# Forgetting attention on one core: the transposes of the inverse sums and the product that spreads them get fixed places behind a tile's scores

## The chip, the core and the metric

The kernel runs as one program on 1 core of one Trainium2 chip. The number that counts is the device time of the whole kernel in microseconds (us). It was run three times before the change, and once more under the profiler.

## What is computed

Two transformer blocks run one behind the other over 1024 tokens of width 1024, in fp32. The second block's mixer holds the part that the change touches, a causal attention with 8 heads of 64 and a forgetting bias, beside a pooling branch:

```python
def forgetting_attention(q, k, v, f_logit):
    ...
    log_f = jax.nn.log_sigmoid(f_logit.astype(jnp.float32)).transpose(0, 2, 1)
    cf = jnp.cumsum(log_f, axis=-1)
    ...
        s = jnp.einsum('bhqd,bhkd->bhqk', qb, k, preferred_element_type=jnp.float32) * scale
        s = s + cq[..., :, None] - cf[..., None, :]
        s = jnp.where(kpos[None, :] <= qpos[:, None], s, NEG_INF)
        p = jax.nn.softmax(s, axis=-1)
        return jnp.einsum('bhqk,bhkd->bhqd', p.astype(v.dtype), v)
```

The rest (retention, window attention, the two MLPs, norms, projections) is long rows of matrix products that the change leaves alone.

## The kernel before

Each engine has its own program, written out by hand, and the programs meet only at semaphores. Products are kept exact to fp32 by splitting operands into a high and a low part.

**Units and items.** The attention is cut into 16 units `u`. Unit `u` belongs to item `idx = u // 2`; items 0 to 7 are (pair of heads `t`, query half `Q`) = (0,0), (0,1), (1,0), and so on, and `j = u % 2` is the head of the pair. So even items have 4 blocks of keys per unit and odd items 8. All engines walk the same list, `attention_order`: 17 steps `s`, each of 4 slots `ii`. In a slot come, in this order, the scores of the tile (128 queries) that follows, the weights of tile (`s`, `ii`), and then, for unit `s - 1`, one turn (even item) or two turns (odd item).

- scores: TensorE (PE) writes them to PSUM (L1049 to L1051), VectorE (DVE) takes their minimum (L2397).
- weights: ScalarE (ACT) takes the exponential into `Pu` (L1667) and adds up the rows into `st`; this frees the scores' bank.
- turn `n`: PE transposes up to 4 blocks of `Pu` into a PSUM bank (L1062), ACT copies that bank to `PAh` (L1675), DVE subtracts to get `PAl` (L2402) and frees the bank. Two turns later PE multiplies `PAh` and `PAl` with the values (L1078, L1079).

**The ring of two banks.** Turns use PSUM banks 4 and 5 in rotation. So a turn's transposes wait for the `PAl` of the turn before the last one, unless something else takes a place in the rotation between them.

**The tail.** When a unit's last values are issued, a generator `tail(u)` starts, and each later turn on each engine takes it one step further. It normalizes the item:

- the first unit of an item, first step on DVE: `inverse`, four small operations (L2415, L2418, L2422, L2423), turns the 8 sums into inverses and packs them into `n4`.
- second step: ACT copies half of the product to `ot` (L1687), DVE adds it to the other half (L2435).
- third step, first unit: PE takes the next bank of the rotation ("nT") and transposes `n4` into it (L1095, 4 transposes, called **the transposes** below); ACT copies the bank to `rw` (L1693) and frees it.
- third step, second unit: PE takes the next bank ("rl") and spreads `rw` over 128 rows with one product (L1103, **the product** below); DVE multiplies the item's output with it (L2440, **the multiplication**) and frees the bank. GpSimd (POOL) then splits the output into `chi` and `clo` (L2659, L2661), in a queue with the operand splits for later pairs of heads (`stack`, L2618 to L2630).

Of the kernel before, what the change touches and what calls it, by code (L numbers as in the profile page):

```python
# [9 lines left out]
ACT = mybir.ActivationFunctionType  # L10
ALU = mybir.AluOpType
# [54 lines left out]
class Tally:  # L66
# [24 lines left out]
    def ok(self, *name):  # L91
        if not self.building:
            return None, 1
        topic, count = self.value[name]
        return self.sem(topic), count
# [110 lines left out]
def idle(n):  # L206

    for _ in range(n):
        yield


def run(gen):
    for _ in gen:
        pass
# [145 lines left out]
ITEMS = [(t, Q) for t in range(4) for Q in range(2)]  # L360
# [9 lines left out]
    return max(0, k - 4 * ITEMS[u // 2][1])  # L370


def attention_order(scores, weights, stack, turned, values, tail, pooled):

    restack, tails = iter(()), []
    scores(0, 0)
    n = 0
    for s in range(17):
        if s % 4 == 1 and s < 12:
            restack = stack(s // 4 + 1)  # L380
        for ii in range(4):
            if 4 * s + ii + 1 < 64:
                scores(*divmod(4 * s + ii + 1, 4))
            if s < 16:
                weights(s, ii)
            next(restack, None)
            if s == 0:
                pooled(ii)
            for _ in range(1 + ITEMS[(s - 1) // 2][1] if s else 0):
                turned(n, *TURNS[n])  # L390
                if n >= LAG:
                    values(n - LAG, *TURNS[n - LAG])
                    if TURNS[n - LAG][0] < TURNS[n - LAG + 1][0]:
                        tails.append(tail(TURNS[n - LAG][0]))
                for g in tails:
                    next(g, None)
                n += 1
    for m in range(n - LAG, n):
        values(m, *TURNS[m])
    tails.append(tail(15))  # L400
    for g in tails:
        run(g)
def build(nc, I, out, sg, cd, yd, xd, ud):
    with ExitStack() as ctx:
        return programs(nc, ctx, I, out, sg, cd, yd, xd, ud)


def programs(nc, ctx, I, out, sg, cd, yd, xd, ud):
    wp, x_in, rows, sinks, bf, ps = (I[n] for n in ("wp_d", "x_d", "rows_d", "sinks_d", "bf_d", "ps_d"))
    cst, swab, poolw, wf = (I[n] for n in ("cst_d", "swab_d", "pw_d", "wf_d"))  # L410
    tally = Tally(nc, ctx)
    up, ok = tally.up, tally.ok
# [5 lines left out]
    def bank_of(*group):  # L418
        return bank[tally.banks[group]]

    def free(*group):

        return tally.sem(f"free{tally.banks[group]}"), 1
# [11 lines left out]
    ident = at("ident", CO, [128, 128])  # L435
# [153 lines left out]
    ov = [at(f"ov{i}", WO + 28 + 2 * i, [128, 512]) for i in range(2)]  # L589
    ot = at("ot", XO + 28, [128, 512])  # L590
    rw = at("rw", XO + 30, [34, 512], F32R)
    sel = at("sel", FO + 72.625, [34, 128], F32R)
    chi4 = at("chi4b", FO, [128, T], F32R)
    nh = at("nh", FO + 72, [128, 8], F32R)
    n4 = at("n4", FO + 72.0625, [128, 136])
# [10 lines left out]
    def unit_of(u):  # L606

        idx, j = divmod(u, 2)
        return (idx, j) + ITEMS[idx]
# [20 lines left out]
    def tensor_program(e):  # L630
        ring = Ring(tally, bank)
# [88 lines left out]
        for q in range(2):  # L720
            P, free = ring.open("vT", q)
# [3 lines left out]
            for j in range(4):  # L725
                t = 4 * q + j
# [118 lines left out]
        for m2 in range(4):  # L845
# [3 lines left out]
            for mm in range(2):  # L849
                m = 2 * m2 + mm  # L850
                for half in range(2):
                    c = slice(512 * half, 512 * half + 512)
                    P, free = ring.open("so", m, half)
# [229 lines left out]
            else:  # L1083
                x.then_inc(*up("val", n))

        def tail(u):
            idx, j, t, Q = unit_of(u)
            yield
            yield
            if j == 0:  # L1090
                P, free = ring.open("nT", idx)
                e.wait_ge(*free)
                e.wait_ge(*ok("n4", idx))
                for ii in range(4):
                    x = e.transpose(P[0:34, 128 * ii:128 * ii + 128], n4[:, 34 * ii:34 * ii + 34], ident[:, :])  # L1095
                x.then_inc(*ring.full("nT", idx))
            else:
                P, free = ring.open("rl", idx)
                e.wait_ge(*free)
                e.wait_ge(*ok("free", "nT", idx))  # L1100
                if idx == 0:
                    e.wait_ge(*ok("n40", 2))
                e.matmul(P[:, :], sel[:, :], rw[:, :], start=True, stop=True).then_inc(*ring.full("rl", idx))  # L1103

        attention_order(scores, nothing, lambda t: idle(8), turned, values, tail, pooled)
        tally.alias(("att_end",), ring.latest)
        ring.turn(range(8))

# [24 lines left out]
    def scalar_program(e):  # L1133
# [546 lines left out]
        def tail(u):  # L1680
            idx, j, t, Q = unit_of(u)
            own, o = rows_of(j)
            yield
            e.wait_ge(*ok("full", "ov", u))
            if u > 1:
                e.wait_ge(*ok("free", "ov", u - 2))
            e.activation(ot[own, :], bank_of("ov", u)[o:o + 64, :], ACT.Copy).then_inc(*up("oal", u))  # L1687
            yield
            if j == 0:
                e.wait_ge(*ok("full", "nT", idx))  # L1690
                if idx:
                    e.wait_ge(*ok("full", "rl", idx - 1))
                e.activation(rw[:, :], bank_of("nT", idx)[0:34, :], ACT.Copy).then_inc(*free("nT", idx))  # L1693

        attention_order(nothing, weights, lambda t: idle(8), turned, nothing, tail, pooled)
        feed.cap = NPIECES
        e.wait_ge(*ok("clo", 7))
        feed.ahead(CAT + 5)
# [33 lines left out]
    def vector_program(e):  # L1732
# [637 lines left out]
        for j in range(2):  # L2370
            o = 64 - 64 * j
# [53 lines left out]
        def tail(u):  # L2425
            idx, j, t, Q = unit_of(u)
            own, _ = rows_of(j)
            o = ov[idx % 2]
            if j == 0:
                inverse(idx)  # L2430
            yield
            e.wait_ge(*ok("oal", u))
            if j == 0 and idx > 1:
                e.wait_ge(*ok("clo", idx - 2))
            e.tensor_tensor(out=o[own, :], in0=bank_of("ov", u)[own, :], in1=ot[own, :], op=ALU.add).then_inc(*free("ov", u))  # L2435
            yield
            if j:
                e.wait_ge(*ok("free", "ov", u))
                e.wait_ge(*ok("full", "rl", idx))
                e.tensor_tensor(out=o[:, :], in0=o[:, :], in1=bank_of("rl", idx)[:, :], op=ALU.mult).then_inc(*free("rl", idx))  # L2440

        attention_order(scores, nothing, lambda t: idle(8), turned, nothing, tail, pooled)
        feed.cap = NPIECES
        feed.ahead(CAT + 5)

# [93 lines left out]
    def pool_program(e):  # L2539
# [108 lines left out]
        run(stack(0))  # L2648
        ones_rows()

        def tail(u):
            idx, j, t, Q = unit_of(u)
            if j == 0:
                return
            c = slice(512 * Q, 512 * Q + 512)
            yield from idle(4)
            e.wait_ge(*ok(*latest))
            e.wait_ge(*ok("free", "rl", idx))
            e.tensor_copy(chi[4 + t][:, c], ov[idx % 2][:, :]).then_inc(*up("cho", idx))  # L2659
            e.wait_ge(*ok("cho", idx))  # L2660
            e.tensor_tensor(out=clo[4 + t][:, c], in0=ov[idx % 2][:, :], in1=chi[4 + t][:, c].bitcast(F32),  # L2661
                            op=ALU.subtract).then_inc(*up("clo", idx))
            latest[:] = "clo", idx

        attention_order(nothing, nothing, stack, nothing, nothing, tail, nothing)
        e.wait_ge(*ok("wt_end", 2))
        e.wait_ge(*ok(*latest))
        e.tensor_copy(chi4[:, :], chi[4][:, :].bitcast(F32)).then_inc(*up("chi4", 0))
# [462 lines left out]
```

## Time and profile before

| | us |
|---|---|
| median of 3 runs | 2570.13 |
| lowest and highest of them | 2567.49 and 2576.94 |
| the profiled execution | 2573.41 |
| its span | 2571.6 |
| PE busy / DVE busy / ACT busy / POOL busy | 2524.5 / 1473.5 / 1056.3 / 189.0 |

The span is the stretch from the first to the last instruction of the profiled execution; the execution's own time is 1.8 us longer. Busy times are sums over the whole span; the attention is a stretch of 138 us in it, from about 1704 to 1842.

### The profile page before, as it was taken

How to read it: one execution, taken by the hardware profiler on the slowest of the kernel's cores; microseconds unless marked ns; L12 is line 12 of the kernel's file. 1: busy time of each engine (PE TensorE's matmuls, PEld its weight loads, DVE VectorE, ACT ScalarE, POOL GpSimd, SP SyncE). 2: the span in 40 equal slices, each digit the busy share in tenths (PEclk: the TensorE clock that was granted, in tenths of full speed). 3: DMA queues.
4: the chain of work that ended last, by engine and by line, in shares of the span. 5: the costliest groups of instructions: out<-in, count | busy, mean ns of one | idle time of the engine just before them, and what ended most of it. 6: DMA issues, size and time to landing. Idle time of an engine off the chain costs nothing.

```text
span 2571.6 us, 30682 instructions
## 1 busy us (share of the span) xinstructions
PE 2524.5 (98%) x12072; PEld 2084.9 (81%) x12072; DVE 1473.5 (57%) x2153; ACT 1056.3 (41%) x1698; POOL 189.0 (7%) x173
## 2 busy tenths in 40 slices
PE   7999999999999999999999999999999999999998
PEld 6777888888888788888888887877788888888886
DVE  4345223323533777666664754358768676576668
ACT  4344322223212544444434543357526444444432
POOL 0000000000020200000000110154111000000000
PEclk9999999999999999999999999999999999999999
DMA  4221211111422426547865541111313464588554
GB/s 165 67 73 66 74 41 42 34 33 66 147 82 82 143 87 218 184 150 260 306 249 183 185 157 59 34 26 34 115 50 131 140 225 137 175 319 327 183 191 166
DMA packets 129679, 347.59 MB, mean 135 GB/s; under 512 B 13152, under 2 KB 13408, under 8 KB 129408
## 3 DMA queue, kind: packets, MB, share of 16 engines
q1 hardware_dynamic: 129536, 345.63, 38.5%
q8 instruction: 96, 1.57, 0.3%
q14 instruction: 47, 0.39, 0.0%
HBM read 256.91 MB, written 85.52 MB: 133 GB/s over the span
## 4 chain that ended last, share of the span: by engine, by line
PE 89%; DVE 5%; issue 3%; DMA 1%; ACT 1%; POOL 1%; SPq 0%; DVEq 0%; ACTq 0%; POOLq 0%
PE bank L635 27%; PE bank L637 27%; PE bank L636 27%; DVE PAl L2402 1%; DVE st L2397 1%; PE bank L696 1%; POOL accX L2584 1%; PE bank L1062 1%; PE bank L746 1%; PE bank L813 1%; DMA rbx<-wp_d 0%; PE bank L817 0%; PE bank L823 0%; PE bank L781 0%; DVE wlo L1735 0%
## 5 line engine op out<-in xcount | busy, mean ns | idle before, releaser
L1735 DVE TENSOR_TENSOR wlo<-raw,whi 128x1024 fp32r<-128x1024 f32 x102 | 125.2, 1235 | 254.1 <-ACT whi L1138 253.4
L635 PE MATMUL bank<-hhi,whi 128*128 128x512 f32 x608 | 249.6, 411 | 1.7 <-DVE hlo L1760 1.7
L637 PE MATMUL bank<-hhi,wlo 128*128 128x512 f32 x608 | 239.3, 394 | 0.0
L636 PE MATMUL bank<-hlo,whi 128*128 128x512 f32 x608 | 238.6, 392 | 0.0
L1138 ACT ACTIVATE whi<-raw 128x1024 fp32r<-128x1024 f32 x102 | 106.6, 1054 | 103.9 <-PE bank L637 88.2
L635 PEld LDWEIGHTS bank<-hhi,whi 128*128 128x128 f32 x608 | 115.1, 189 | 29.0 <-issue 6.7
L637 PEld LDWEIGHTS bank<-hhi,wlo 128*128 128x128 f32 x608 | 114.9, 189 | 25.2
L636 PEld LDWEIGHTS bank<-hlo,whi 128*128 128x128 f32 x608 | 115.3, 190 | 22.3
L1443 ACT ACTIVATE r<-r 128x512 f32<-128x512 f32 x78 | 49.1, 629 | 137.6 <-DVE r L2220 100.0
L635 PE MATMUL bank<-yhi,whi 128*128 128x512 f32 x192 | 75.0, 391 | 0.0
L637 PE MATMUL bank<-yhi,wlo 128*128 128x512 f32 x192 | 74.8, 390 | 0.0
L636 PE MATMUL bank<-ylo,whi 128*128 128x512 f32 x192 | 74.8, 390 | 0.0
L635 PE MATMUL bank<-whi,hhi 128*128 128x256 f32 x256 | 74.4, 290 | 0.0
L636 PE MATMUL bank<-wlo,hhi 128*128 128x256 f32 x256 | 72.5, 283 | 0.0
L637 PE MATMUL bank<-whi,hlo 128*128 128x256 f32 x256 | 72.5, 283 | 0.0
L635 PE MATMUL bank<-uw0bh,uw0ah 128*128 128x512 f32 x176 | 68.9, 391 | 0.8 <-DVE uw0bl L2172 0.7
L636 PE MATMUL bank<-uw0bl,uw0ah 128*128 128x512 f32 x176 | 68.6, 390 | 0.0
L637 PE MATMUL bank<-uw1bh,uw1al 128*128 128x512 f32 x176 | 68.6, 390 | 0.0
L637 PE MATMUL bank<-uw0bh,uw0al 128*128 128x512 f32 x176 | 68.6, 390 | 0.0
L635 PE MATMUL bank<-uw1bh,uw1ah 128*128 128x512 f32 x176 | 68.6, 390 | 0.0
L636 PE MATMUL bank<-uw1bl,uw1ah 128*128 128x512 f32 x176 | 68.6, 390 | 0.0
L2593 POOL TENSOR_TENSOR accX<-accX,acc 128x1024 f32<-128x1024 f32 x8 | 20.2, 2519 | 609.7 <-DVE acc L2279 609.7
(477 smaller groups left out, 7206.6 us busy)
## 6 DMA issues: line engine op xcount, KB each, us to landing
ra<-ud_d SPq DMA_DIRECT2D x112, 512.0 KB, 4.5
raw<-wp_d SPq DMA_DIRECT2D x102, 512.0 KB, 3.5
rbh<-wp_d SPq DMA_DIRECT2D x64, 512.0 KB, 5.7
rawp<-wp_d SPq DMA_DIRECT2D x26, 1024.0 KB, 5.8
ud_d<-us SPq DMA_DIRECT2D x104, 256.0 KB, 5.4
rbw<-wp_d SPq DMA_DIRECT2D x48, 512.0 KB, 3.6
ud_d<-f SPq DMA_DIRECT2D x76, 256.0 KB, 2.0
rbx<-wp_d SPq DMA_DIRECT2D x32, 512.0 KB, 7.6
```

Source lines behind the costliest of these rows:

```text
L635: e.matmul(P, sh, mh, start=first, stop=False, skip_group_check=more)
L636: e.matmul(P, sh, ml, start=False, stop=False, skip_group_check=more)
L637: return e.matmul(P, sl, mh, start=False, stop=last, skip_group_check=more)
L696: i = e.transpose(P[:, 128 * j:128 * j + 128], src[:, 128 * k:128 * k + 128], ident[:, :])
L746: i = e.matmul(P[:, 256 * (m % 2) + j0:256 * (m % 2) + 256], qs[64 * g:64 * g + 64, m, 128 * n:128 * n + 128], ks[64 * g:64 * g + 64, 128 ...
L813: x = e.matmul(P[:, 0:256], ss[n % 2][:, :], rv[i][:, n, :], start=True, stop=n == 0)
L1062: x = e.transpose(P[:, 128 * ii:128 * ii + 128], Pu[u % 2][ii][:, 128 * k:128 * k + 128], ident[:, :])
L1138: e.activation(whi[n % SLOTS][:, :], raw[n % RAWS][:, :], ACT.Copy).then_inc(*up("whi", n))
L1443: e.activation(r[:, :], r[:, :], ACT.Relu).then_inc(*up("relu", tag, name, p))
L1735: e.tensor_tensor(out=wlo[n % SLOTS][:, :], in0=raw[n % RAWS][:, :], in1=whi[n % SLOTS][:, :].bitcast(F32), op=ALU.subtract).then_inc(*up( ...
L2397: e.tensor_reduce(st[:, m:m + 1], psum[:, b:b + w], AXIS.X, ALU.min).then_inc(*up("mn", u, ii))
L2402: e.tensor_tensor(out=PAl[n % 3][:, c], in0=bank_of("pt", n)[:, c], in1=PAh[n % 3][:, c].bitcast(F32), op=ALU.subtract).then_inc(*free("pt ...
```

## The change

Transposes, `rw` copy, product, multiplication and the split on POOL leave the tails. They become two functions, `rows` and `spread`, called from fixed places of `attention_order`: `rows(idx)` at the even step `s = 2 idx + 2`, slot 2, and `spread(idx)` at the odd step `s = 2 idx + 3`, slot 3, both behind the scores and weights of the slot and ahead of its turns. The last item's `spread` stays at the very end. `inverse`, the copy to `ot` and the addition stay where they were.

```diff
-def attention_order(scores, weights, stack, turned, values, tail, pooled):
+def attention_order(scores, weights, stack, turned, values, tail, rows, spread, pooled):
...
             if s < 16:
                 weights(s, ii)
+            if ii == 2 and s > 1 and s % 2 == 0:
+                rows(s // 2 - 1)
+            if ii == 3 and s > 2 and s % 2:
+                spread((s - 3) // 2)
             next(restack, None)
...
     for g in tails:
         run(g)
+    spread(7)
...
-        def tail(u):
-            idx, j, t, Q = unit_of(u)
-            yield
-            yield
-            if j == 0:
-                P, free = ring.open("nT", idx)
...
-        attention_order(scores, nothing, lambda t: idle(8), turned, values, tail, pooled)
+        def rows(idx):
+            P, free = ring.open("nT", idx)
+            e.wait_ge(*free)
+            e.wait_ge(*ok("n4", idx))
+            for ii in range(4):
+                x = e.transpose(P[0:34, 128 * ii:128 * ii + 128], n4[:, 34 * ii:34 * ii + 34], ident[:, :])
+            x.then_inc(*ring.full("nT", idx))
+
+        def spread(idx):
+            P, free = ring.open("rl", idx)
+            e.wait_ge(*free)
+            e.wait_ge(*ok("free", "nT", idx))
+            if idx == 0:
+                e.wait_ge(*ok("n40", 2))
+            e.matmul(P[:, :], sel[:, :], rw[:, :], start=True, stop=True).then_inc(*ring.full("rl", idx))
...
+        def rows(idx):
+            e.wait_ge(*ok("full", "nT", idx))
+            if idx:
+                e.wait_ge(*ok("full", "rl", idx - 1))
+            e.activation(rw[:, :], bank_of("nT", idx)[0:34, :], ACT.Copy).then_inc(*free("nT", idx))
...
+        def spread(idx):
+            o = ov[idx % 2]
+            e.wait_ge(*ok("free", "ov", 2 * idx + 1))
+            e.wait_ge(*ok("full", "rl", idx))
+            e.tensor_tensor(out=o[:, :], in0=o[:, :], in1=bank_of("rl", idx)[:, :], op=ALU.mult).then_inc(*free("rl", idx))
```

What this does to the order of instructions depends on the item's parity, since an even item has one turn per slot and an odd item two.

On PE, at the transposes of item 4 (an even item), the kernel before has them behind the last turn of slot 3. `Pu` and `ident` are a turn's transposes, `n` is the packed inverses, `KH`/`KM` with `QS`/`QM` are scores, `PAh`/`PAl` with `vrest` the values:

```order
L1062 MATMUL bank<-ident,Pu_326 128x128
L1078 MATMUL bank<-PAh_328,vrest 128x512
L1079 MATMUL bank<-PAl_331,vrest 128x512
L1049 MATMUL bank<-KH_292,QS_288 128x512
L1050 MATMUL bank<-KM_300,QM_296 128x512
L1049 MATMUL bank<-KH_292,QS_288 128x128
L1050 MATMUL bank<-KM_300,QM_296 128x128
L1051 MATMUL bank<-maskb,identb 128x128
L1062 MATMUL bank<-ident,Pu_326 128x128
L1078 MATMUL bank<-PAh_329,vrest 128x384
L1079 MATMUL bank<-PAl_332,vrest 128x384
L1095 MATMUL bank<-ident,n_340 34x128 x4
```

Now they stand ahead of the turn of slot 2 (`Pu_325`, `Pu_326`):

```order
L1057 MATMUL bank<-maskb,identb 128x128
L1097 MATMUL bank<-ident,n_340 34x128 x4
L1068 MATMUL bank<-ident,Pu_325 128x128
L1068 MATMUL bank<-ident,Pu_326 128x128
L1084 MATMUL bank<-PAh_328,vrest 128x512
L1085 MATMUL bank<-PAl_331,vrest 128x512
L1055 MATMUL bank<-KH_292,QS_288 128x512
L1056 MATMUL bank<-KM_300,QM_296 128x512
L1055 MATMUL bank<-KH_292,QS_288 128x128
L1056 MATMUL bank<-KM_300,QM_296 128x128
L1057 MATMUL bank<-maskb,identb 128x128
```

So the turns of slots 2 and 3, two pairs of value products and one tile's scores that stood ahead of the transposes now stand behind them.

On ACT, at the same place of item 4, the copy to `rw` stood behind the last turn's copy; `Pu` are the weights, `PAh` the turns' copies, `ot` the half of the output:

```order
L1667 ACTIVATE Pu_321,st<-bank,st 128x896
L1675 ACTIVATE PAh_327<-bank 128x256
L1687 ACTIVATE ot<-bank 64x512
L1667 ACTIVATE Pu_322,st<-bank,st 128x1024
L1675 ACTIVATE PAh_328<-bank 128x128
L1693 ACTIVATE rw<-bank 34x512
L1667 ACTIVATE Pu_323,st<-bank,st 128x640
```

Now it stands ahead of the turn's copy of slot 2, and of the weights of the 1024 keys wide tile:

```order
L1670 ACTIVATE Pu_321,st<-bank,st 128x896
L1696 ACTIVATE rw<-bank 34x512
L1678 ACTIVATE PAh_327<-bank 128x256
L1690 ACTIVATE ot<-bank 64x512
L1670 ACTIVATE Pu_322,st<-bank,st 128x1024
L1678 ACTIVATE PAh_328<-bank 128x128
L1670 ACTIVATE Pu_323,st<-bank,st 128x640
```

So the weights of the widest tile, which stood two places ahead of the `rw` copy, now stand three places behind it.

On PE, at the product of item 5 (an odd item), the product stood behind the turn and the values of slot 3; `rw` with `sel` is the product:

```order
L1051 MATMUL bank<-maskb,identb 128x128
L1062 MATMUL bank<-ident,Pu_322 128x128
L1078 MATMUL bank<-PAh_328,vrest 128x384
L1079 MATMUL bank<-PAl_331,vrest 128x384
L1103 MATMUL bank<-rw,sel 128x512
L1049 MATMUL bank<-KH_293,QS_289 128x512
```

Now it is ahead of that turn:

```order
L1057 MATMUL bank<-maskb,identb 128x128
L1106 MATMUL bank<-rw,sel 128x512
L1068 MATMUL bank<-ident,Pu_322 128x128
L1084 MATMUL bank<-PAh_328,vrest 128x384
L1085 MATMUL bank<-PAl_331,vrest 128x384
L1055 MATMUL bank<-KH_293,QS_289 128x512
```

So the turn and the product have changed places in the rotation of the two banks. At the transposes of an odd item only the scores of one tile and the transposes change places, and at the product of an even item the product moves two turns later.

## Rows read from the trace of the kernel before

**Rows 1.** Page, part 4: the chain that ended last, by engine.
```profile
PE 89%; DVE 5%; issue 3%; DMA 1%; ACT 1%; POOL 1%; SPq 0%; DVEq 0%; ACTq 0%; POOLq 0%
```

**Rows 2.** Busy times in the attention (start:end, length, engines, PE clock, DMA).
```profile
1704.00:1842.12 138.12, 125.89 (x763) 95.69 (x761) 118.14 (x215) 107.09 (x244) 58.59 (x62) 0.98 0.13 32
```

**Rows 3.** Waits in the attention, 1704 to 1842 (us, times, longest).
```profile
PEld bank L1095 <- DVE PAl L2402: 9.5, 8, 1.8
...
PE bank L1095 <- DVE PAl L2402: 6.6, 7, 1.3
...
PE bank L1049 <- ACT Pu L1667: 2.5, 9, 0.4
```

**Rows 4.** Timeline around the transposes of item 4 (start, length, engine).
```profile
1783.23 0.39 PE L1062 MATMUL bank<-ident,Pu 128*128 128x128 f32 x2
1783.27 1.10 DVE L2418 CAST nh<-st 128x8 fp32r<-128x8 f32 x1
...
1783.69 0.37 ACT L1675 ACTIVATE PAh<-bank 128x256 fp32r<-128x256 f32 x1
...
1784.09 0.59 ACT L1687 ACTIVATE ot<-bank 64x512 f32<-64x512 f32 x1
...
1784.49 0.59 DVE L2423 TENSOR_TENSOR n<-st,nh 128x8 f32<-128x8 f32 x1
...
1785.00 1.21 DVE L2397 TENSOR_REDUCE st<-bank 128x1 f32<-128x1024 f32 x1
...
1786.24 1.11 ACT L1667 ACTIVATE Pu<-bank,st 128x1024 f32<-128x1024 f32 x1 [1.56 <-DVE st L2397]
...
1786.60 0.61 PE L1095 MATMUL bank<-ident,n 128*34 128x128 f32 x4 [1.31 <-DVE PAl L2402]
...
1787.50 0.50 PE L1049 MATMUL bank<-KH,QS 128*128 128x512 f32 x1 [0.29 <-ACT Pu L1667]
1787.50 0.58 ACT L1693 ACTIVATE rw<-bank 34x512 fp32r<-34x512 f32 x1
```

**Rows 5.** Timeline, the same place of item 6.
```profile
1816.74 0.39 PE L1062 MATMUL bank<-ident,Pu 128*128 128x128 f32 x2
...
1817.06 0.16 DVE L2423 TENSOR_TENSOR n<-st,nh 128x8 f32<-128x8 f32 x1
...
1819.64 0.50 PE L1049 MATMUL bank<-KH,QS 128*128 128x512 f32 x1 [0.29 <-ACT Pu L1667]
```

**Rows 6.** Timeline, the same place of item 2.
```profile
1748.28 1.06 ACT L1138 ACTIVATE whi<-raw 128x1024 fp32r<-128x1024 f32 x1
...
1748.79 0.59 DVE L2423 TENSOR_TENSOR n<-st,nh 128x8 f32<-128x8 f32 x1
...
1751.80 0.59 PE L1049 MATMUL bank<-KH,QS 128*128 128x512 f32 x1 [0.29 <-ACT Pu L1667]
```

**Rows 7.** Timeline around the transposes of item 5.
```profile
1802.39 0.62 PE L1095 MATMUL bank<-ident,n 128*34 128x128 f32 x4 [0.30 <-DVE PAl L2402]
...
1802.85 0.67 DVE L2402 TENSOR_TENSOR PAl<-bank,PAh 128x512 fp32r<-128x512 f32 x1
...
1803.58 0.66 PE L1062 MATMUL bank<-ident,Pu 128*128 128x128 f32 x4
```

**Rows 8.** Timeline around the product of item 5.
```profile
1812.80 0.29 DVE L2402 TENSOR_TENSOR PAl<-bank,PAh 128x128 fp32r<-128x128 f32 x1
...
1813.01 0.68 DVE L2440 TENSOR_TENSOR ov<-ov,bank 128x512 f32<-128x512 f32 x1
...
1813.15 0.66 PE L1062 MATMUL bank<-ident,Pu 128*128 128x128 f32 x4
```

**Rows 9.** Timeline, last turn of the step behind item 4's product.
```profile
1797.17 0.27 PE L1062 MATMUL bank<-ident,Pu 128*128 128x128 f32 x1
```

**Rows 10.** Busy times behind the transposes of item 2; the PE clock is third from the end.
```profile
1751.00:1753.00 2.00, 1.71 (x8) 1.17 (x7) 2.00 (x3) 1.39 (x4) 0.00 (x0) 0.77 0.07 13
1753.00:1755.00 2.00, 1.83 (x10) 1.60 (x9) 1.38 (x3) 1.18 (x3) 0.00 (x0) 0.50 0.00 0
```

More of the change, by code:

```diff
@@ L1084, in values @@
                 x.then_inc(*up("val", n))
-        def tail(u):
-            idx, j, t, Q = unit_of(u)
-            yield
-            yield
-            if j == 0:
-                P, free = ring.open("nT", idx)
[L1092 to L1103, printed above, removed]
-        attention_order(scores, nothing, lambda t: idle(8), turned, values, tail, pooled)
+        def rows(idx):
[12 more added lines that the diff above has]
+            e.matmul(P[:, :], sel[:, :], rw[:, :], start=True, stop=True).then_inc(*ring.full("rl", idx))
+        attention_order(scores, nothing, lambda t: idle(8), turned, values, lambda u: idle(2), rows, spread, pooled)
         tally.alias(("att_end",), ring.latest)
@@ L1687, in tail @@
             e.activation(ot[own, :], bank_of("ov", u)[o:o + 64, :], ACT.Copy).then_inc(*up("oal", u))
[L1688 to L1695, printed above, removed]
+        def rows(idx):
[3 more added lines that the diff above has]
+            e.activation(rw[:, :], bank_of("nT", idx)[0:34, :], ACT.Copy).then_inc(*free("nT", idx))
+        attention_order(nothing, weights, lambda t: idle(8), turned, nothing, tail, rows, nothing, pooled)
         feed.cap = NPIECES
@@ L2435, in tail @@
             e.tensor_tensor(out=o[own, :], in0=bank_of("ov", u)[own, :], in1=ot[own, :], op=ALU.add).then_inc(*free("ov", u))
[L2436 to L2442, printed above, removed]
+        def spread(idx):
[3 more added lines that the diff above has]
+            e.tensor_tensor(out=o[:, :], in0=o[:, :], in1=bank_of("rl", idx)[:, :], op=ALU.mult).then_inc(*free("rl", idx))
+        attention_order(scores, nothing, lambda t: idle(8), turned, nothing, tail, nothing, spread, pooled)
         feed.cap = NPIECES
@@ L2649, in pool_program, with spread @@
         ones_rows()
[L2651 to L2654, printed above, removed]
+        def spread(idx):
+            t, Q = ITEMS[idx]
             c = slice(512 * Q, 512 * Q + 512)
-            yield from idle(4)
             e.wait_ge(*ok(*latest))
@@ L2663, in tail @@
             latest[:] = "clo", idx
-        attention_order(nothing, nothing, stack, nothing, nothing, tail, nothing)
+        attention_order(nothing, nothing, stack, nothing, nothing, lambda u: idle(2), nothing, spread, nothing)
         e.wait_ge(*ok("wt_end", 2))
```

## The prediction

> **What bounds the kernel now.** I read the page first. The chain of waits that ends last runs over PE for 89% of the span [rows 1]: whatever lengthens or shortens PE's own queue moves the end, and what only moves another engine does not. The change touches nothing outside the attention, so next I asked for the busy times of that stretch. It lasts 138.12 us, PE is busy for 125.89 of them and DVE for 118.14 [rows 2]. So PE idles for 12.2 us there, and DVE is nearly as full: this stage is a loop over PE, ACT and DVE, in which whoever waits for PE's result is soon waited for by PE.
>
> Third, the list of waits. The largest item on PE is the one that the change goes for: ahead of the transposes (L1095) the matmul side idles for 6.6 us, at 7 of the 8 places, until DVE has written a `PAl` and so freed the bank (9.5 us on the weight load side). PE's wait for the weights of a tile, ahead of scores (L1049), is 2.5 us in all [rows 3]. On the face of it up to 6.6 us are to be had. Whether they are depends on what ends last if that wait goes, and for that I read the timeline around single places. They fall in two kinds.
>
> **Transposes of even items (0, 2, 4, 6), the main term.** At item 4, PE idles 1.31 us, does the transposes at 1786.60, then idles 0.29 us more until ACT is through with the widest tile's weights and starts the scores at 1787.50 [rows 4]. Those scores need the weights' bank whatever stands before them. The weights (1786.24, idle before it 1.56 us) wait for DVE's minimum of 1.21 us at 1785.00, which stands behind `inverse` [rows 4]. So the chain is inverse, minimum, weights, scores. The transposes lie in a gap of it, and taking their wait away returns nothing here.
>
> The move puts them on that chain. PE now comes to them behind the scores of slot 2, at 1783.23, where the turn now starts, and has to wait for `n4`, which `inverse` finishes at 1784.49 + 0.59 = 1785.08 [rows 4]. PE stands still for 1.85 us with the turn behind it. From there: transposes 0.61, to about 1785.70; `rw` copy 0.58, to 1786.3; the turn's copy `PAh` 0.37, to 1786.7; `ot` 0.59, to 1787.3; and only then the widest tile's weights, since ACT works in order. They start at 1787.35 where they started at 1786.24. That is **1.1 us** later, and the scores behind them with it: 1788.6 for 1787.50. DVE had slack for one minimum only (its `PAl` and addition now also come 0.6 to 0.9 us later, but before the new start of the scores matters to it). I find nothing behind that absorbs it: in the trace PE is not idle again until the next item's transposes.
>
> Item 0's rows read like item 4's, so 1.1 again. Item 6 has a fast `inverse` (`n4` at 1817.06 + 0.16 = 1817.22), but PE gets there at 1816.74 [rows 5], and the same sum of lengths from `n4` on gives weights that end at about 1820.65, against scores that started at 1819.64: 1.05. At item 2 a piece of the weights for the next stage, 1.06 us on ACT at 1748.28, stands between `PAh` and `ot` [rows 6]. Before, it ran while ACT would have waited; behind the `rw` copy it lies on the chain too. `n4` is there at 1749.38, then 0.61 + 0.58 + 0.37 + 1.06 + 0.59 and the weights of 1.2 lead to 1753.9, against 1751.80: 2.1 later. But in the old run the steps behind it waited for DVE as well, so part is hidden: I take 1.6, between 1.1 and 2.1. Sum of the four: 1.1 + 1.6 + 1.1 + 1.05 = **+4.85 us**.
>
> **Transposes of odd items (1, 3, 5, 7).** Item 5: PE idles 0.30 us, transposes at 1802.39, then the scores, then the next turn at 1803.58. That turn starts as the `PAl` of 1802.85 ends (1803.52) [rows 7]. With the scores ahead, PE fills the wait with them and does the transposes behind; but the turn still waits for the same `PAl`, which depends on DVE alone. Items 1 and 3 have the same shape. At item 7 no scores are left, so nothing moves. The `rw` copy falls into ACT's wait for PE. **0 us**; if the next turn had not been held, it would be up to the idle time itself, 0.3 to 0.7 us an item.
>
> **The product of odd items (1, 3, 5).** Before, the turn behind the product used the bank whose `PAl` ended at 1813.09 and started at 1813.15. Now it takes the product's bank, which is free only when the multiplication has run. DVE does the multiplication (0.68) [rows 8] where the short `PAl` stood, so the bank comes free about 0.2 to 0.3 us later, and ACT's copy and the next weights follow. 3 x 0.2 = **+0.6 us**. Item 7's product stays at the end.
>
> **The product of even items (0, 2, 4, 6).** Two turns move 0.4 us earlier, then the product stands ahead of the last two turns, and the very last one needs its bank: multiplication done at about 1797.15, where that turn started at 1797.17 [rows 9]. 0 for three of them; at item 6, where fewer scores stand in between, 0.2 us may be gained: **-0.2 us**.
>
> **POOL and the DMA queue.** The splits behind an odd item's multiplication come two operand splits earlier in POOL's queue, so two of `stack`'s steps now wait for it. The operands that they make are used more than 10 us later, so I cost this at nothing. It shifts which POOL operation runs during `inverse`, though. The small cast took 1.10 us at item 4 [rows 4], and at item 6 the last of the four operations took 0.16 instead of 0.59 [rows 4, 5], where POOL had nothing to do. That can move `n4` by 0.4 us either way at items 2 and 4, which goes into the range.
>
> **Sum.** 4.85 + 0 + 0.6 - 0.2 = +5.25 us. The profiled execution took 2573.41, so it would be 2578.7. The median of the runs shown lies 3.3 lower; on its scale the forecast is 2570.1 + 5.3 = 2575.4 us, a ratio of 1.002. The three runs spread over 9.4 us, so half a percent, 12.9 us, is about what a measurement of this kernel can tell from no change. My forecast is a small loss that reads as no change.
>
> **Rivals.**
>
> *A gain: the wait was the cost (chance 0.13).* If PE's arrival decides and not DVE's, the 6.6 us of idle time ahead of the transposes [rows 3] go, to 2563.5. For it: the profile names this wait as PE's largest here. Against it: at even items the scores wait a further 0.29 us for ACT, and at odd items the turn starts within 0.1 us of its `PAl` [rows 4, 7]. It would decide if `n4` were ready before PE comes, which takes an `inverse` that ends 1.85 us earlier.
>
> *Nothing moves (0.17).* If ACT reorders its slack better than my sum has it (each of the four chains is short by one operation, about 0.6 us, and item 2 hides all of its piece), the loss is below 2.5 us and the median lies at 2570 to 2572.5.
>
> *Longer stops cost the clock (0.15).* Behind item 2's transposes the granted clock was 0.77 of full speed over 2 us and 0.50 over the next 2 [rows 10]: PE had stood still ahead of the transposes (up to 1.3 us [rows 3]) and once more ahead of the scores, and went from its level of 2.4 GHz to that of 1.2 GHz. A mean of 0.77 and 0.50 is some 2.9 us at half speed, which loses about 1.5 us each time. At items 0, 4 and 6 it did not happen. The new stops ahead of the transposes (1.85 us without any work) may add up to three of these, 4.5 us, which makes 2580. Against it: the stop is now cut in two, with work between. The Trainium skill, TensorE: Matmul & The Clock Gate, section "A second HAM failure mode: psum-queue depth-cycling", describes short PE pauses between groups of matmuls that cycle through PSUM banks as enough to make the clock swing between its two levels; this trace agrees at one even item of four. By that rule every even item would pay, which is this rival's time.
>
> *A real loss, over 12.9 us (0.04).* It needs all of the above at their upper ends and a late operand for the next pair of heads.
>
> **How the numbers follow.** The forecast, a loss of 2.5 to 8 us, has a chance of 0.51. Its own range is 2572.5 to 2578. The range reaches down to part of the gain and up to the clock's case, with the scatter of a median of few runs: 2566 to 2583. Nearly all cases lie within 12.9 us of 2570.1: faster 0.02, the same 0.93, slower 0.05.
>
> **What the profile will show.** Right: the transposes' wait at even items is for `inverse` or its packing (DVE L2423 by its old line), some 1.8 us at items 0, 2 and 4 and 0.5 at item 6; the widest tile's weights on ACT start about 2.2 us after `n4`; the attention takes 5 us more. At odd items the wait ahead of the transposes is gone and stands ahead of the next turn instead. Wrong: if the attention is no longer than 138 us, the chain through `rw` and `ot` was not what held the weights; if it is over 8 us longer, look at the clock first.

## The result and the profile after

The changed kernel takes **2574.35 us** (median of 21 runs, 2571.93 to 2576.56), the kernel before 2569.02 us (median of 21, 2566.58 to 2576.94). The medians differ by 5.3 us. The ratio on record, with its 95% interval, is not their quotient: it is 1.0017 (1.001 to 1.0023), a loss of 4.4 us (2.6 to 5.9). Either way the loss is well inside half a percent, and yet the interval excludes no change.

The chain that ended last runs over PE for 91% of the span (the page's part 4), where it was 89% [rows 1]:

```profile
PE 91%; DVE 4%; issue 2%; ACT 1%; POOL 1%; DMA 0%; SPq 0%; DVEq 0%; ACTq 0%; POOLq 0%
```

The waits of the changed kernel in the attention, 1704 to 1850 (us in all, times, longest), answer to [rows 3]:

```profile
ACT rw L1696 <- PE bank L1097: 8.0, 7, 1.7
...
PE bank L1097 <- DVE n L2426: 5.4, 4, 1.8
PE bank L1055 <- ACT Pu L1670: 5.4, 6, 1.9
...
PE bank L1097 <- DVE PAl L2405: 2.5, 3, 1.3
...
PE bank L1106 <- DVE PAl L2405: 1.5, 4, 0.6
PE bank L1068 <- DVE ov L2444: 1.2, 3, 0.4
```

PE waited 6.6 us for `PAl` ahead of the transposes [rows 3]; now 2.5 are left of that, at the odd items, and 5.4 us stand there for `n`, the end of `inverse`, at exactly four places: the even items. PE's wait for weights ahead of scores went from 2.5 us to 5.4. The 1.2 us for DVE L2444 are new: three turns that wait until the multiplication has freed the product's bank.

From the start of the first turn to the last product, the trace of before has 137.34 us (1704.78 to 1842.12), that of after 141.75 (1702.60 to 1844.35). The length of this stretch is what I compare below as "the attention". The 2.18 us by which it starts earlier lie ahead of everything that the change touches, and what follows the last product is 1.9 us shorter (727.5 us for 729.5). Together they are the reason why the two profiled executions (2573.41 and 2573.65 us) look alike while the medians do not. In the eleven traces of this case the attention starts anywhere from 1701.5 to 1705.4 us: one execution scatters by as much as the effect, so only the stretch of the change can be read from it.

The chain of the forecast is to be seen at item 4 (timeline of the changed kernel: start, length, engine), beside [rows 4]:

```profile
1785.04 0.48 DVE L2421 CAST nh<-st 128x8 fp32r<-128x8 f32 x1
...
1786.09 0.16 DVE L2426 TENSOR_TENSOR n<-st,nh 128x8 f32<-128x8 f32 x1
1786.17 1.21 DVE L2400 TENSOR_REDUCE st<-bank 128x1 f32<-128x1024 f32 x1
...
1786.39 0.60 PE L1097 MATMUL bank<-ident,n 128*34 128x128 f32 x4 [1.49 <-DVE n L2426]
...
1787.03 0.59 ACT L1696 ACTIVATE rw<-bank 34x512 fp32r<-34x512 f32 x1 [1.47 <-PE bank L1097]
...
1787.52 0.36 ACT L1678 ACTIVATE PAh<-bank 128x256 fp32r<-128x256 f32 x1
...
1787.91 0.59 ACT L1690 ACTIVATE ot<-bank 64x512 f32<-64x512 f32 x1
...
1788.53 1.11 ACT L1670 ACTIVATE Pu<-bank,st 128x1024 f32<-128x1024 f32 x1
...
1789.79 0.50 PE L1055 MATMUL bank<-KH,QS 128*128 128x512 f32 x1 [0.94 <-ACT Pu L1670]
```

`n` ends at 1786.25. The transposes, `rw`, `PAh` and `ot` follow one another without a gap, and the weights of the widest tile start at 1788.53, 2.28 us after `n`. The minimum that they waited for before (1.56 us idle [rows 4]) is now done at 1787.38, 1.15 us before they start.

### The profile page after: what moved, and what is told of

The parts are those of the page before. It is cut to its first block, busy times and chain, and to the rows that moved or that the text cites. A ratio compares the mean times of both kernels' runs of the same rounds, so it can differ in the third digit from the quotient of the medians.

```text
span 2571.9 us, 30682 instructions
## 1 busy us (share of the span) xinstructions
PE 2520.0 (98%) x12072; PEld 2082.6 (81%) x12072; DVE 1475.6 (57%) x2153; ACT 1057.8 (41%) x1698; POOL 189.9 (7%) x173
## 4 chain that ended last, share of the span: by engine, by line
PE 91%; DVE 4%; issue 2%; ACT 1%; POOL 1%; DMA 0%; SPq 0%; DVEq 0%; ACTq 0%; POOLq 0%
PE bank L641 28%; PE bank L643 28%; PE bank L642 28%; DVE PAl L2405 1%; PE bank L702 1%; DVE st L2400 1%; PE bank L1068 1%; POOL accX L2588 1%; PE bank L752 1%; PE bank L819 1%; PE bank L823 0%; PE bank L829 0%; PE bank L787 0%; ACT PAh L1678 0%; DVE wlo L1738 0%
```

## The experiments

To be able to move one part at a time, the order is generated in the nine kernels from a few constants: `ROWS_AT` is the slot in whose place the transposes and the `rw` copy stand (even items, odd items), `SPREAD_AT` the same for the product, the multiplication and POOL's split; `None` is the old place, behind a turn. The change itself is (2, 2) and (3, 3). Each median is that of 11 runs, beside 21 to 33 runs of the kernel before in the same sitting; the changed kernel was not run again in these sittings. As above, a ratio can differ from the quotient of its medians by some hundredths of a percent. One run of e3 took 6726 us; the median isn't moved by it, and its ratio leaves it out.

### One part of the change alone (e1 to e4)

```
e1  ROWS_AT = (2, 2)        SPREAD_AT = (None, None)   transposes alone
e2  ROWS_AT = (None, None)  SPREAD_AT = (3, 3)         product alone
e3  ROWS_AT = (None, 2)     SPREAD_AT = (None, None)   transposes of odd items alone
e4  ROWS_AT = (3, 2)        SPREAD_AT = (None, None)   transposes of even items one tile later
```

> The transposes and the rw copy at their new places, the product and the multiplication still in the tails. My theory (the even items' transposes wait for the inverses and put themselves, the rw copy and ot ahead of the widest tile's weights) expects nearly the whole loss: +4 to +5 us over the kernel before, PE waiting 1.5 to 1.8 us ahead of the transposes at items 0, 2, 4. The rival, that the loss comes from the product taking the bank of the next turn, expects 0 to +1 us.

> The product, the multiplication and POOL's splits at their new places, the transposes still in the tails. My theory expects +0.4 to +1.2 us (three odd items at 0.2 to 0.4, even items near 0), with a turn that waits 0.4 us for the multiplication behind each odd item's product. The rival that blames the product expects +4 us or more.

> Only the odd items' transposes at their new place, all else as before. My theory expects 0, within 0.5 us: the wait of 0.3 to 0.7 us ahead of the transposes goes and comes back ahead of the next turn, which waits for the same PAl. The rival, that such a wait is a cost of its own, expects a gain of 1.5 to 2 us (the idle times at items 1, 3 and 5 together).

> Even items' transposes one slot later than in the change: behind the scores of slot 3 and ahead of its turn, with rw behind the widest tile's weights; odd items' as in the change, the product as before. My theory expects the loss to vanish: within 1 us of the kernel before, no wait for the inverses, since they are packed by then and rw no longer stands ahead of the weights. The rival, that any place behind the scores costs, expects +4 us.

| kernel | median us | before us | ratio, 95% interval | attention us | with low clock |
|---|---|---|---|---|---|
| before | | | | 137.34 | items 2, 7 |
| after | 2574.35 | 2569.02 | 1.0017, 1.001 to 1.0023 | 141.75 | item 2 |
| e1 | 2573.76 | 2569.96 | 1.002, 1.0011 to 1.0029 | 141.26 | item 2 |
| e2 | 2569.14 | 2569.96 | 0.9996, 0.9987 to 1.0005 | 135.75 | none |
| e3 | 2570.48 | 2569.96 | 0.9997, 0.9988 to 1.0006 | 137.45 | items 2, 7 |
| e4 | 2569.07 | 2569.96 | 0.9996, 0.9987 to 1.0004 | 134.99 | none |

The last column says where the profiled execution ran at the low clock for a stretch (see below). e1 carries the loss; e2 and e3 carry none that can be measured. e1 moves all transposes, e3 those of the odd items alone, so the loss is the move of the even items' transposes. PE waits 1.72, 1.78 and 1.79 us ahead of those of items 0, 2 and 4 in e1, as I had expected. e4 shows that it is not the move as such but how far it goes: one tile later, and the loss is gone. At item 4 of e4 (timeline of e4; its lines stand 12 further down than those of the changed kernel):

```profile
1782.95 0.60 PE L1109 MATMUL bank<-ident,n 128*34 128x128 f32 x4 [0.38 <-DVE n L2438]
...
1783.97 1.11 ACT L1682 ACTIVATE Pu<-bank,st 128x1024 f32<-128x1024 f32 x1 [1.53 <-DVE st L2412]
...
1785.08 0.58 ACT L1708 ACTIVATE rw<-bank 34x512 fp32r<-34x512 f32 x1
...
1785.23 0.50 PE L1067 MATMUL bank<-KH,QS 128*128 128x512 f32 x1 [0.23 <-ACT Pu L1682]
```

The weights wait for the minimum again, as before, and `rw` stands behind them. PE's waits ahead of all transposes add up to 2.1 us in e4 (1.3 for `PAl`, 0.8 for `n`), where they were 6.6 [rows 3]. They came back elsewhere: PE's wait for `PAl` ahead of the next turns, 1.9 us in the kernel before, is the largest of e4:

```profile
PE bank L1080 <- DVE PAl L2417: 5.9, 11, 0.8
```

So of those 4.5 us hardly any was time to be had. The time of e4 does not exclude a small gain (its interval goes from 3.3 us less to 1.0 more). The attention lengths seem to say that e2 and e4 gain 1.6 and 2.4 us; most or all of that is the clock (below): the trace of before has two stretches at the low level, theirs none.

For the odd items, e3's trace (PE at item 5) shows the wait only moved, from ahead of the transposes (0.30 us [rows 7]) to ahead of the next turn:

```profile
1800.39 0.60 PE L1109 MATMUL bank<-ident,n 128*34 128x128 f32 x4
...
1801.52 0.66 PE L1080 MATMUL bank<-ident,Pu 128*128 128x128 f32 x4 [0.53 <-DVE PAl L2417]
```

### The inverse earlier (e5, e6)

```
     # DVE, in attention_order, ahead of the turns of slot 0
+    if s > 1 and s % 2 == 0 and ii == 0:
+        first(s // 2 - 1)              # inverse(idx)
     # DVE, in the tail of the item's first unit
-    if j == 0:
-        inverse(idx)
```

e5 is this in the kernel before, e6 in the changed kernel. If PE's stop for `n` is the whole cost, e6 takes it away.

> The kernel before with DVE's inverse called one or two turns earlier, at the start of the step (slot 0, ahead of its turns) instead of in the tail. My theory says that at even items the chain is PAl, inverse, minimum of the widest tile, weights, scores, so taking 0.7 to 2 us of inverse out of it gives the chain time back, unless DVE pays for it at slot 0, where it is as full. I expect a gain of 1 to 4 us. The rival, that DVE is the bound of the whole stage, expects 0.

> The changed kernel with the same early inverse. If PE's wait for the inverses is what the change costs, it goes: I expect the loss against the kernel before to shrink from 5.3 us to 0 to 2 us, and the wait ahead of the even items' transposes to vanish. If instead the rw copy and ot ahead of the widest tile's weights cost by themselves, some 3 to 4 us of the loss stay.

e5: 2570.03 us beside 2570.09, ratio 1.0 (0.9991 to 1.0009), attention 136.51. e6: 2571.36 beside 2570.09, ratio 1.0001 (0.9992 to 1.001), attention 138.98, with a stretch of low clock at item 2. By the times e6 has shrunk the loss to 1.3 us (medians) or 0.3 (ratio; −2.1 to 2.6), as I had expected it if PE's wait were the cost. Its one trace shows less of that, but it also shows which waits are left. In e6 the wait ahead of the even items' transposes is gone (what is left at item 0, 0.25 us, is for `PAl`), and with it 2.8 us of the attention, half of what the change had added once the clock is left out (5.6, below). What is left (PE of e6, items 2 and 4):

```profile
1748.95 0.61 PE L1109 MATMUL bank<-ident,n 128*34 128x128 f32 x4
...
1750.41 0.44 PE L1080 MATMUL bank<-ident,Pu 128*128 128x128 f32 x2 [0.85 <-DVE PAl L2417]
...
1754.62 0.51 PE L1067 MATMUL bank<-KH,QS 128*128 128x512 f32 x1 [2.11 <-ACT Pu L1682]
...
1785.59 0.61 PE L1109 MATMUL bank<-ident,n 128*34 128x128 f32 x4
...
1787.05 0.44 PE L1080 MATMUL bank<-ident,Pu 128*128 128x128 f32 x2 [0.85 <-DVE PAl L2417]
...
1790.31 0.50 PE L1067 MATMUL bank<-KH,QS 128*128 128x512 f32 x1 [1.15 <-ACT Pu L1682]
```

PE waits for weights longer than in the changed kernel (6.3 us in all, 5.4 there), and a turn has begun to wait for DVE, which now does `inverse` where it had a `PAl` to write. So in this trace PE's stop for `n` and the late weights are two things, and removing the first alone does not bring the second back. How much of the loss stays with the late weights is open: the trace says 2.8 us, the times say less. e5 missed what I had expected of it, a gain; its attention, without low clock, is even 1.2 us longer than that of before without its own (135.3, below). Its PE (item 4) shows why:

```profile
1783.03 0.51 PE L1067 MATMUL bank<-KH,QS 128*128 128x512 f32 x1 [1.22 <-ACT Pu L1682]
...
1784.32 0.60 PE L1109 MATMUL bank<-ident,n 128*34 128x128 f32 x4
...
1785.15 0.50 PE L1067 MATMUL bank<-KH,QS 128*128 128x512 f32 x1 [0.24 <-ACT Pu L1682]
```

The stop ahead of the transposes (1.31 us [rows 4]) is gone, and one of 1.22 us stands ahead of the scores one tile earlier, since DVE's operations before them now come later by the length of `inverse`. I take it that DVE has the same work to do by the time of these weights wherever `inverse` stands in it; no run separates this.

### The chain through ot (e7)

```
     # ACT, tail of a unit, ahead of the copy to ot; DVE likewise, ahead of its addition
+    if not j and not Q:
+        yield
```

At even items `ot` and DVE's addition now run one turn later (the two were moved together), so on ACT `ot` stands behind the widest tile's weights and no longer ahead of them. PE's order is that of the changed kernel, its stop for `n` included.

> The changed kernel with ot of an even item's first unit (ACT, 0.59 us) and the addition on DVE one turn later, so that ot is behind the widest tile's weights. It shortens the new chain on ACT by one operation. My theory expects 0.5 us less per even item, 1.5 to 2.4 us off the changed kernel. The rival, that PE's stop ahead of the transposes alone is the cost, expects no change against the changed kernel.

Median 2571.07 us beside 2570.09, ratio 1.0005 (0.9996 to 1.0014), attention 137.89 and no low clock in it, 3.9 us shorter than after, of which some 0.8 to 0.9 are after's stretch of low clock. Item 4 in its timeline:

```profile
1783.99 0.60 PE L1109 MATMUL bank<-ident,n 128*34 128x128 f32 x4 [1.48 <-DVE n L2440]
...
1784.62 0.59 ACT L1710 ACTIVATE rw<-bank 34x512 fp32r<-34x512 f32 x1 [1.45 <-PE bank L1109]
...
1785.12 0.36 ACT L1690 ACTIVATE PAh<-bank 128x256 fp32r<-128x256 f32 x1
...
1785.38 1.10 ACT L1682 ACTIVATE Pu<-bank,st 128x1024 f32<-128x1024 f32 x1
...
1786.62 0.50 PE L1067 MATMUL bank<-KH,QS 128*128 128x512 f32 x1 [0.19 <-ACT Pu L1682]
1786.76 0.60 ACT L1704 ACTIVATE ot<-bank 64x512 f32<-64x512 f32 x1
```

The stop ahead of the transposes is as long as in the changed kernel (1.48 us, 1.49 there), but the scores' wait falls from 0.94 us to 0.19. At all four even items the scores come 0.76 or 0.77 us sooner behind the transposes than in the changed kernel, some 3 us together; I had expected 1.5 to 2.4. This shows the mechanism in the trace: with an unchanged stop of PE, what is taken off ACT between `rw` and the weights comes back. The intervals of e7 and of the changed kernel overlap, so the times alone would not show it.

### POOL's second piece of splitting later (e8, e9)

```
-SPLIT_TURNS = (30, 89)
+SPLIT_TURNS = (39, 89)
```

This moves the piece for the next stage (`whi` on ACT, `wlo` on DVE) away from item 2's transposes. e8 is the changed kernel with it, e9 is e4 with it.

> The changed kernel with the weight piece that stands in item 2's chain (1.06 us on ACT, 1.2 us on DVE) moved from turn 30 to turn 39, the last of item 3's first unit, ahead of which ACT and DVE wait for PE. My theory says that this piece lies on the new chain between PAh and ot: item 2's step shrinks to what item 4's is, about 1 us less in the attention, so +3.5 to +4.5 us over the kernel before. The rival, that the piece is hidden at either place, expects +5.3 us as in the change.

> The even items' transposes in slot 3, the odd ones' in slot 2, the product as before, and the piece at turn 39 too. I expect a gain of 1 to 2.5 us on the kernel before, 0.5 to 1 us more than without the moved piece; if DVE is the bound of the stage, the piece costs the same at turn 39 and the result is that of the version without it.

e8: 2573.87 us beside 2570.76, ratio 1.0011 (1.0002 to 1.002), attention 141.21, with a stretch of low clock at item 7 and none at item 2; without it about 140.0 (worked out below). e9: 2568.63 beside 2570.76, ratio 0.9989 (0.9979 to 0.9998), attention 135.18. So about 0.9 us of the loss in the trace (140.9 without its low clock) comes from the piece, and at item 2 the scores follow the transposes after 3.40 us, where it had been 4.34: the piece did lie on the chain. The loss is 3.1 us by the medians and 4.7 by the trace, on either side of the 3.5 to 4.5 that I had expected; the medians are too coarse to show one piece. e9 is the only kernel whose interval lies below 1, and by a tenth of a percent (2.1 us by the medians, inside the 1 to 2.5 that I had expected). Its trace does not explain this by the piece (135.18 us, e4 134.99); I take it as e4's result once more. Where its gain would come from is not shown: without the clock its attention is as long as that of before.

## Why the prediction held, by its own steps

Each step can be measured as the shift of after against before from one anchor on PE to the next (here the scores behind the even items' transposes, the turns behind the odd ones and behind the products). The first anchor is the first turn, at −2.18 us. In the table the starts are of before and after.

| step | anchors before / after | measured us | forecast us |
|---|---|---|---|
| item 0, transposes | 1717.96 / 1716.88 | +1.10 | +1.1 |
| item 1, transposes | 1734.42 / 1733.75 | +0.41 | 0 |
| item 1, product | 1743.97 / 1743.71 | +0.41 | +0.2 |
| item 2, transposes | 1751.80 / 1753.00 | +1.46 | +1.6 |
| item 3, transposes | 1770.09 / 1771.44 | +0.15 | 0 |
| item 3, product | 1779.65 / 1781.41 | +0.41 | +0.2 |
| item 4, transposes | 1787.50 / 1789.79 | +0.53 | +1.1 |
| item 5, transposes | 1803.58 / 1805.84 | −0.03 | 0 |
| item 5, product | 1813.15 / 1815.80 | +0.39 | +0.2 |
| item 6, transposes | 1819.64 / 1823.41 | +1.12 | +1.05 |
| item 6, product | 1836.76 / 1840.20 | −0.33 | −0.2 |
| to the last product | 1842.12 / 1844.35 | −1.21 | 0 |

Up to the last row the sum is +5.62 us, the forecast was +5.25, the medians differ by 5.3 and the ratio says 4.4. That the sum comes so close is in part luck: its terms were off in both directions (the main one by −0.6, item 1 by +0.4, the product of odd items by +0.6).

**The main term** was right as a mechanism (e1, e4 and e7 show it) and near in its sum, 4.21 for 4.85. Items 0 and 6 come out to 0.1 us. At item 4 it was half. The steps behind `n` took what I had added up (2.28 us from `n` to the weights; 2.2 said), but `inverse` itself was shorter, 1.44 us from first to last operation where it had been 2.04: its cast took 0.48 us at 1785.04, where it had taken 1.10 [rows 4]. So PE stood still for 1.49 us and not for 1.85. I had named this as an uncertainty of 0.4 us either way and put it into the range only; it was 0.6.

e1, where POOL's splits stay at their old place, shows the four steps by themselves. Its `inverse` is as long as before (casts of 1.07 and 1.06 us at items 2 and 4), and from anchor to anchor it loses 1.1, 2.1, 1.1 and 1.1 us. So the 1.6 us that I took for item 2 was right by luck. The part that I called hidden was not hidden: the full sum of 2.1 came out in e1. In the changed kernel an `inverse` shorter by 0.6 us brought it down to 1.46.

Here is item 2 after, beside [rows 6]:

```profile
1747.33 0.49 DVE L2421 CAST nh<-st 128x8 fp32r<-128x8 f32 x1
...
1747.94 0.58 DVE L2426 TENSOR_TENSOR n<-st,nh 128x8 f32<-128x8 f32 x1
...
1748.66 0.60 PE L1097 MATMUL bank<-ident,n 128*34 128x128 f32 x4 [1.47 <-DVE n L2426]
...
1750.06 1.05 ACT L1141 ACTIVATE whi<-raw 128x1024 fp32r<-128x1024 f32 x1
...
1751.75 1.11 ACT L1670 ACTIVATE Pu<-bank,st 128x1024 f32<-128x1024 f32 x1
...
1753.00 0.60 PE L1055 MATMUL bank<-KH,QS 128*128 128x512 f32 x1 [1.88 <-ACT Pu L1670]
```

From `n` (1748.52) to the weights are 3.23 us: item 4's 2.28 and nearly the whole length of `whi`, 1.05. The fall of `inverse` comes with the move of the product and of POOL's split: e2, where these move alone, has casts of 0.51 us at both items.

**Transposes of odd items**: 0 was right within 0.15 us at items 3 and 5, and in e3, where they are moved alone (ratio 0.9997). The 0.41 us at item 1 are not theirs: e1 and e3 have nothing there, e2 has 0.40. They come with the product and POOL's split, which I had costed at nothing outside items 2 and 4. `inverse` now meets POOL's operations differently at item 1 (cast 0.57 and subtraction 0.58 us, 0.17 and 0.16 before, all four 1.49 for 1.03), and DVE is what the next turn waits for.

**The product of odd items** was mis-sized: 0.4 us each, not 0.2, together 1.2 for 0.6. The mechanism is as forecast, and its price is simply PE's new wait for the multiplication (timeline of the changed kernel, item 1):

```profile
1742.96 0.69 DVE L2444 TENSOR_TENSOR ov<-ov,bank 128x512 f32<-128x512 f32 x1
...
1743.57 0.28 DVE L2405 TENSOR_TENSOR PAl<-bank,PAh 128x128 fp32r<-128x128 f32 x1
...
1743.71 0.55 PE L1068 MATMUL bank<-ident,Pu 128*128 128x128 f32 x3 [0.41 <-DVE ov L2444]
```

I had compared only DVE's two ends (0.68 for 0.29 us in one place, so 0.2 to 0.3 later) and left out what PE no longer waits for: before, it got to that turn just as the bank came free, so the whole lateness shows. **The product of even items** was right in its sum (−0.33 for −0.2 at item 6), though PE now waits 0.3 to 0.6 us for `PAl` ahead of each (L1106 above), which I had not foreseen. e2, where the products and POOL's splits move alone, has an attention of 135.75 us, 0.4 longer than that of before without its low clock; that is less than the rows above add up to. I read it as the shorter `inverse` giving part back: PE waits 0.71 us ahead of the transposes of items 2 and 4 in e2, where it had been 1.28 and 1.31.

**The rivals.** The gain (6.6 us of idle time given back) fell: PE idles more than before, 18.9 of 138 us where it was 12.2 of 138.12 [rows 2], as the busy times of the changed kernel show:

```profile
1704.00:1842.00 138.00, 119.10 (x742) 93.10 (x740) 116.84 (x208) 105.78 (x237) 58.06 (x61) 0.99 0.13 32
```

And e4, which takes away most of the wait that was to be gained, has an attention only 0.3 us shorter once the clock is left out. "Nothing moves", a loss below 2.5 us, fell by the interval (2.6 to 5.9 us), if only just. A loss over 12.9 us fell by it as well. The clock's rival fell too: it asked for up to three more stretches at the lower level, at items 0, 4 and 6, and the new stops there (1.75, 1.49 and 0.73 us) brought none; the trace of after has one stretch at the low level, at item 2, that of before two. I had also overlooked the second one of before, at item 7, and priced a stretch at 1.5 us, where it costs 0.8 to 1.2 (below). What I drew from the Trainium skill, TensorE: Matmul & The Clock Gate, section "A second HAM failure mode: psum-queue depth-cycling", that every even item would pay, is thus not borne out by the traces of this kernel.

**The last row** of the table is that clock. In the trace of before, PE fell to the 1.2 GHz level once behind item 2's transposes [rows 10] and once more behind item 7's; in that of after, only behind item 2's. The two traces at item 7 (2 us each; PE clock third from the end), first before, then after:

```profile
1836.00:1838.00 2.00, 1.43 (x9) 0.94 (x8) 0.71 (x2) 1.14 (x2) 0.00 (x0) 0.85 0.54 213
1838.00:1840.00 2.00, 2.00 (x9) 1.70 (x8) 1.25 (x2) 0.54 (x2) 0.00 (x0) 0.50 0.00 0
1840.00:1842.00 2.00, 1.89 (x10) 1.39 (x9) 0.72 (x2) 0.66 (x2) 0.00 (x0) 0.79 0.00 0
```

```profile
1838.00:1840.00 2.00, 0.61 (x4) 0.31 (x4) 1.97 (x6) 0.57 (x2) 0.00 (x0) 1.00 0.54 129
1840.00:1842.00 2.00, 1.80 (x11) 1.35 (x11) 0.62 (x2) 1.16 (x3) 0.00 (x0) 1.00 0.36 141
1842.00:1844.00 2.00, 1.85 (x11) 1.23 (x10) 1.49 (x4) 0.84 (x3) 0.00 (x0) 1.00 0.00 0
```

At item 7 both orders are the same up to the last turns, and the stop ahead of the transposes is 1.32 or 1.33 us in nine of the eleven traces (0.73 in e5, 0.31 in e6). From the transposes to the last product it takes 6.54 to 6.57 us where the clock falls (before, e3, e8) and 5.33 or 5.34 in the other eight: 1.2 us a time. At item 2 the changed kernel takes 18.44 us from the scores behind the widest tile's weights to the turn behind item 3's transposes, and e7 and e8, whose traces keep the full clock there, 17.64 and 17.67: 0.8 us. In the kernel before PE falls 0.9 us behind e2 during the stretch, of which 0.5 are left behind item 3's transposes. I take 0.8 to 0.9 for this stretch, so the lengths without low clock are good to some tenths of a us: about 135.3 us before and 140.9 after, a difference of 5.6, where the medians say 5.3.

What stays open is how often these stretches come in the other executions, and whether the order of instructions changes that. At item 2 the traces of before, after, e1, e3 and e6 have the stretch and the six others have none; each version has one trace, so this may be the version or chance, and taking the stretches out as I do assumes that it is chance. Against before, the medians of seven of the nine experiments lie 0.6 to 1.6 us lower than their traces without low clock lie against 135.3 (e2: −0.8 by the medians, +0.4 by the trace; e7: +1.0 and +2.6). e9 lies 2.0 lower, e3 0.4 higher. That would fit a kernel before that pays for a stretch in most of its executions. The granted clocks on record lean the same way: on average 0.9985 for e2 and 0.9968 for the kernel before beside it, where one stretch is worth 0.0007. But four traces (e3, e5, e7, e8) also have low clock in the first 30 us, far from the attention, so this does not settle it.

## What to carry to other kernels

A wait that the profile names is worth what the next one leaves of it: before moving an instruction out of a wait, follow the engine's next instruction to its own releaser; if that one would have been the last to come anyway, the wait is free space, and what stands in it costs nothing there. When a short operation moves ahead on one engine, every in-order engine that follows its result moves its own part too: here a copy of 0.59 us on ACT, which nobody waited for, got ahead of the one operation of 1.1 us that everybody waits for. One step later (e4) the same move costs nothing, so try the neighbouring places before giving a placement up; and compare the stretch of the change, not spans, when the effect is as small as the scatter of one execution.

## What the runs showed of the hardware

- **Tiny DVE operations beside POOL.** `inverse` is four operations on 128x8 tiles. The eleven traces hold 88 of its casts. In 46 of them a POOL operation was running when the cast began and outlasted its 0.17 us; these took 0.48 to 1.12 us, and every one ended 0.02 to 0.04 us behind that POOL operation. The other 42 took 0.17 or 0.18 us. For instance, in the kernel before, POOL's subtraction ran from 1783.06 for 1.29 us, to 1784.35, and the cast that began at 1783.27 ended at 1784.37 [rows 4]. The Trainium skill, SBUF — State Buffer, section "SBUF: two separate sides", says that DVE and GpSimd share a port for which they contend; these rows agree. The price for an operation of 0.17 us is up to six times its length.
- **Stretches at the low clock.** They come singly and last about 3.4 us (in the three rows of before above the clock falls short of full speed by 0.15, 0.50 and 0.21 over 2 us each, which is 3.4 us at half speed). The same code with the same stop of PE ahead of it (1.32 or 1.33 us at item 7) had one in the profiled executions of before, e3 and e8 and none in those of after, e1, e2, e4, e7 and e9. The stops of 1.49 to 1.75 us at items 0 and 4 of the changed kernel were followed by none. So a single profile does not tell whether a version pays for one, and two attentions are compared only after the rows of the clock have been looked at.
